# Two more decoder layers: four extra thirds of weight products inside the grouped attention, and another matmul order in the value products

## The reference, cut to what matters

```
u    = rms_norm(h)
proj = u @ w_in                       # dq dk dv | rq rk rv rg | gq gk gv | gates
a = differential_attention(dq, dk, dv)     # 4 heads, values of width 128
r = bidirectional_retention(rq, rk, rv)    # 4 heads, values of width 128, gated by rg
c = grouped_query_attention(gq, gk, gv)    # 8 query heads, 2 key heads
merged = sum over n of sigmoid(gate_n) * (branch_n @ w_branch[n])
h = h + merged @ w_out
h = h + square(relu(rms_norm(h) @ w_mlp_in)) @ w_mlp_out
```

## Time and profile before

| | us |
|---|---|
| median of 3 runs (2966.72 to 2968.79) | 2968.23 |
| the profiled execution, own time | 2965.84 |
| its span, first to last instruction | 2964.0 |
| PE busy in the span | 2915.3 |
| mean granted clock of TensorE | 0.995 of full |

### The profile page before, as it was taken

How to read it: one execution, slowest core, us unless ns; L and a number is a source line. 1 busy time by engine, 2 the same in 40 slices (tenths; PEclk the granted TensorE clock), 3 DMA queues, 4 the chain that set the end, 5 groups by cost and what they waited for, 6 DMA issues and landing times. The chain is left out here.

```text
span 2964.0 us, 36309 instructions
## 1 busy us (share of the span) xinstructions
PE 2915.3 (98%) x13287; PEld 2309.0 (78%) x13287; DVE 1561.3 (53%) x2043; ACT 1276.1 (43%) x1892; POOL 484.3 (16%) x284
## 2 busy tenths in 40 slices
PE   9999999999999999999999999999999999999999
PEld 7787778888788877577777888887667777888887
DVE  4437668345864667656643541445655744553341
ACT  3556325334533446645543431234654554332221
POOL 5002300000100002211112222222221111222121
PEclk9999999999999999999999999999999999999999
DMA  7322213333333332123323333333122322333332
GB/s 192 91 72 70 59 50 97 95 100 94 105 91 101 94 97 67 48 79 89 90 72 93 93 99 94 97 100 100 49 66 72 108 71 78 99 94 98 99 93 93
DMA packets 468595, 263.04 MB, mean 89 GB/s; under 512 B 29674, under 2 KB 457564, under 8 KB 468448
## 3 DMA queue, kind: packets, MB, share of 16 engines
q1 hardware_dynamic: 462512, 250.09, 29.6%
q0 software_dynamic: 5936, 11.03, 1.3%
HBM read 253.70 MB, written 5.64 MB: 87 GB/s over the span
## 5 line engine op out<-in xcount | busy, mean ns | idle before, releaser
L780 POOL TENSOR_TENSOR wL<-wR,wH 128x1024 fp32r<-128x1024 f32 (+1 forms) x165 | 400.6, 2429 | 2265.3 <-ACT wH L742 2265.2
L742 ACT ACTIVATE wH<-wR 128x1024 fp32r<-128x1024 f32 (+3 forms) x472 | 489.0, 1036 | 419.9 <-DMA wR<-in_w_mlp_out_dram 196.5
L747 DVE TENSOR_TENSOR wL<-wR,wH 128x1024 fp32r<-128x1024 f32 (+2 forms) x307 | 372.2, 1212 | 416.3 <-ACT wH L742 392.9
L822 PE MATMUL ps<-uH,wH 128*128 128x512 f32 x1184 | 485.2, 410 | 0.2 <-ACT dts L1732 0.2
L822 PE MATMUL ps<-uL,wH 128*128 128x512 f32 x1184 | 464.8, 393 | 0.0
L809 PE MATMUL ps<-uH,wH 128*128 128x512 f32 x976 | 382.5, 392 | 2.1 <-ACT wH L742 2.1
L809 PE MATMUL ps<-uL,wH 128*128 128x512 f32 x976 | 379.8, 389 | 0.0
L822 PE MATMUL ps<-uH,wL 128*128 128x512 f32 x1184 | 306.8, 401 | 0.0
L822 PEld LDWEIGHTS ps<-uH,wH 128*128 128x128 f32 x1184 | 223.9, 189 | 68.0 <-issue 23.0
L809 PE MATMUL ps<-mH,wH 128*128 128x512 f32 x688 | 267.9, 389 | 0.0
L809 PE MATMUL ps<-mL,wH 128*128 128x512 f32 x688 | 267.7, 389 | 0.0
(11 more groups left out here) (487 smaller groups left out, 4129.0 us busy)
## 6 DMA issues: line engine op xcount, KB each, us to landing
wR<-in_w_in_dram SPq DMA_DIRECT2D x182, 512.0 KB, 3.8
wR<-in_w_mlp_in_dram SPq DMA_DIRECT2D x64, 512.0 KB, 4.0
wR<-in_w_mlp_out_dram SPq DMA_DIRECT2D x64, 512.0 KB, 4.0
wR<-in_ffn_w_up_dram SPq DMA_DIRECT2D x44, 512.0 KB, 3.8
wR<-in_w_branch_dram SPq DMA_DIRECT2D x16, 512.0 KB, 3.4
wR<-in_w_out_dram SPq DMA_DIRECT2D x16, 512.0 KB, 4.1
wR<-in_ffn_w_down_dram SPq DMA_DIRECT2D x16, 384.0 KB, 3.4
wR<-in_ffn_w_down_dram SPq DMA_DIRECT2D x16, 320.0 KB, 3.0
```

What stands on the lines that cost most here:

```text
L742: st.f(st.e.activation(wH[:, slot, 0:n], wR[:, slot, 0:n], ACT.Copy), hi_ready, c + 1)
L747: st.f(st.e.tensor_tensor(wL[:, slot, 0:n], wR[:, slot, 0:n], wH[:, slot, 0:n].bitcast(F32), ALU.subtract), lo_ready, c + 1 if done is Non ...
L780: e.tensor_tensor(wL[:, slot, 0:n], wR[:, slot, 0:n], wH[:, slot, 0:n].bitcast(F32), ALU.subtract).then_inc(sem("lo_pool"), 1)
L822: ins = pe.matmul(o[:, :], w[:, k, :], x[:, k, :], start=s == 0, stop=s == 3 * KD - 1)
```

## The change

In `gqa_steps` the fill behind the transposes takes two thirds instead of one in the four steps with a value product (u = 6, 10, 14, 18), so the grouped attention takes 42 thirds of the stream and not 38, every later step finds the stream up to four thirds further on, and 28 thirds are left behind the retention instead of 32. In `v_pe` the order within a chunk becomes: both high-weight passes of all four token tiles (16 matmuls), then the wait for wL, then the eight low-weight matmuls. A token tile's group is therefore closed in the last eight matmuls of the last chunk.

```diff
 def gqa_steps(score, turned, value, vturn, fill):
@@
         if 2 <= u < 18:
             turned(u - 2)
-        fill(1)
+        fill(2 if u >= 6 and u % 4 == 2 else 1)
         if u == 1:
             vturn()
@@ def v_pe(pe, kind, l, rotated):
             slot = use(pe, (kind, j), l)
-            use_low(pe, (kind, j), l)
             h, lo = wk(wH, slot, kt, cols), wk(wL, slot, kt, cols)
-            for t, g in enumerate(groups):
-                o = g.open(pe) if j == 0 else g.ps
-                for s in range(3 * kt):
-                    k, (w, u) = s // 3, ((h, uH), (h, uL), (lo, uH))[s % 3]
-                    x = j * kt + k
-                    ins = pe.matmul(o[:, 0:cols], u[:, x, t * P:(t + 1) * P], w[:, k, :],
-                                    start=x == 0 and s == 0, stop=x == KD - 1 and s % 3 == 2)
-                    if s == 3 * kt - 1 and j == n - 1:
-                        g.close(ins)
-                    if s == 3 * kt - 1 and j < n - 1 and t == NT - 1:
-                        ins.then_inc(w_part, 1)
-                    if j == 0 and t == NT - 1 and s == 3 * kt - 1:
-                        rope_post_pe(pe, rotated, len(TILES[rotated]) - 1, l)
-                    if (6 * t + s) % THIRD == THIRD - 1:
-                        yield
+            steps = [(t, k, w, u) for t in range(NT) for k in range(kt) for w, u in ((h, uH), (h, uL))]
+            steps += [(t, k, lo, uH) for t in range(NT) for k in range(kt)]
+            for s, (t, k, w, u) in enumerate(steps):
+                g, x = groups[t], j * kt + k
+                first, last = k == 0 and w is h and u is uH, w is lo and k == kt - 1
+                if j == 0 and first:
+                    g.open(pe)
+                if s == 2 * NT * kt:
+                    use_low(pe, (kind, j), l)
+                ins = pe.matmul(g.ps[:, 0:cols], u[:, x, t * P:(t + 1) * P], w[:, k, :],
+                                start=j == 0 and first, stop=j == n - 1 and last)
+                if j == n - 1 and last:
+                    g.close(ins)
+                if s == len(steps) - 1 and j < n - 1:
+                    ins.then_inc(w_part, 1)
+                if j == 0 and s == len(steps) - 1:
+                    rope_post_pe(pe, rotated, len(TILES[rotated]) - 1, l)
+                if s % THIRD == THIRD - 1:
+                    yield
```

## The result

The changed kernel takes 2979.58 us (median of 5 runs, 2979.38 to 2983.63) against 2968.23 before (2966.6 to 2969.62): ratio 1.0045, 95% interval 1.0034 to 1.0055. It is slower by 11.4 us; 2980.5 was predicted. The span of the profiled execution went from 2964.0 to 2977.7 us, 13.7 more, as the one profiled before was on the short side of its runs.

What follows compares the result with a forecast made beforehand. PE's instruction stream was taken as the bound, busy 2915.3 of 2964.0 us. Per layer 6.0 wait + 2.5 clock - 2.3 gain = 6.2, twice 12.4, on 2968.23 gives 2980.6; predicted 2980.5, range 2972.5 to 2987.

Steps and rivals of the forecast that it cites:

- The tail's cover: Behind the retention's last `var`: four thirds gone, PE waits 6.0 us per layer for brL, bounds 4.7 and 7.3.
- The clock: Behind the new wait at the branch chunk: half clock costs 2.5 us per layer, bounds 0 and 3.4.
- The sentence that the edit can only change the 49 us without work: Whole kernel: with no matmul added or removed, only the 49 us in which PE is not busy can change.
- The gain: Grouped attention: added thirds fill waits of PE and win 2.3 us per layer, bounds 0 and 5.7.
- the two short places: Grouped attention's bank rotation: waits of 0.82 and 1.34 us at steps 9 and 12 move to 7 and 11, left standing.
- The value product: New matmul order in the value chunks: nothing won or lost; if the cover is short, up to 2.7 us per layer.
- no new row at line 2840: Value product, table of PE's waits: no new wait there was named as a sign of a right prediction.
- The rival of the shared port: Grouped attention: DVE operations slowed beside POOL's subtractions take back 2.8 us per layer, so no gain; 2985.2 us, chance 0.16.
- The clock did not stay at full: Behind the branch chunk's wait: rival claimed full clock, so 7.4 us slower in all, 2975.6 us; chance 0.13.
- the grouped attention did not give back all its idle time: Waits behind step 6: rival claimed all 5.7 us per layer won, 2973.8 us, just within 0.2%; chance 0.10.

Runs made afterwards that it cites:

- experiment 1: Kernel before plus only the four extra thirds in the grouped attention, value products in the old order: 2980.62 us, ratio 1.0051.
- experiment 2: Kernel before plus only the new order of the value products, one third per step as before: 2967.0 us, ratio 1.0000.
- experiment 3: Changed kernel, but the differential attention gives four thirds back, so 32 are again left behind the retention: 2969.16 us, ratio 1.0011.
- 5: Changed kernel with two extra thirds per layer (steps 6 and 14) instead of four: 2967.89 us, ratio 1.0006.
- experiment 6: Changed kernel, but ScalarE and VectorE handle the last head's norm ahead of the gate chunk ending just before it: 2977.15 us, ratio 1.0039.
- experiment 4: Changed kernel with 22 unused matmuls ahead of the first branch chunk of merge n = 1 in each layer: 2976.85 us, ratio 1.0036.
- experiment 7: Kernel before with four extra thirds at the value products, four fewer in the differential attention, old value-product order: 2964.42 us, ratio 0.9994.
- experiment 8: Kernel before with extra thirds in step 0, behind step 6's transposes, ahead of those of 7 and 11; differential attention four fewer: 2960.99 us, ratio 0.9981.

## Why the prediction was right

**The tail's cover, shown.** The step that decided, four thirds taken from in front of a chain of 7.6 us, held in place and size: 6.0 us forecast, 5.77 measured, twice. The chain itself was 7.63 us against the 7.64 read from the second head; the forecast of 6.0 differs because the profile counts the idle time from the end of the matmul ahead (1583.28 + 0.39) and not from its next start. Experiments 1 and 2 put the loss with the thirds, 3 removes it by giving the cover back, 5 shows that it follows the cover, 6 splits the chain as read.

**The clock, right in kind, too large.** 2.5 us per layer were taken from a gap of 4.76 us; 1.4 and 1.75 were measured (experiment 4). The row gave the length of the half clock from the moment work resumed. In its gap the clock was at 0.83 on average:

```profile
265.60:270.20 4.60, 0.00 (x0) 0.00 (x0) 2.29 (x2) 3.00 (x5) 3.96 (x3) 0.83 0.28 85
```

Here it was at 0.50 for the last 3.0 us of the first layer's wait, so less work fell into the half clock (3.0 and 3.7 us, not 5.0). How much falls behind the wait differs from one place to the next, from 1.4 us to the 2.8 of experiment 6; one row could not give the size, and only the bounds of 0 and 3.4 held. The sentence that the edit can only change the 49 us without work leaves this term out: behind the wait the work itself took longer (0.79 us for the first matmul instead of 0.39).

**The gain, too large as well.** 2.3 us per layer were forecast. The bgL wait of 1.56 us went, and the two short places came back at steps 7 and 11 as counted. But they cost 1.6 to 1.7 us each and not 0.82 and 1.34. PE asks for the bank 4.5 us after the score's start at all four places; what differs is when DVE takes the row maxima of that score. Timelines of PE and of DVE before, for scores 8 and 11:

```profile
1209.04 1.13 PE L3122 MATMUL ps<-qk_g 64*128 64x256 f32 x8 [0.37 <-ACT gpr L3186]
...
1233.56 1.13 PE L3122 MATMUL ps<-qk_g 64*128 64x256 f32 x8
```

```profile
1211.94 1.49 DVE L3220 TENSOR_REDUCE stt<-ps 128x1 f32<-128x512 f32 x2
...
1236.95 1.49 DVE L3220 TENSOR_REDUCE stt<-ps 128x1 f32<-128x512 f32 x2
```

Timelines of PE and of DVE after, for score 10 (score 6 starts at 1195.46, above):

```profile
1229.23 1.14 PE L3125 MATMUL ps<-qk_g 64*128 64x256 f32 x8
```

```profile
1195.26 1.45 DVE L3053 TENSOR_TENSOR qk_d<-raw,cs_d 128x512 f32<-128x512 f32 x1
...
1199.18 1.49 DVE L3223 TENSOR_REDUCE stt<-ps 128x1 f32<-128x512 f32 x2
...
1232.91 1.48 DVE L3223 TENSOR_REDUCE stt<-ps 128x1 f32<-128x512 f32 x2
```

The maxima come 2.90 and 3.39 us after the score's start before, 3.72 and 3.68 after: 0.82 and 0.29 more, and the waits grew by 0.85 and 0.28. Scores 6 and 10 stand in steps with a value product, 8 and 11 do not: after, DVE does bgL (1194.42 and 1228.15) and then the four operations of a "d" tile's rotation (from 1195.26 at score 6) ahead of the maxima. That this order is the reason is read from the rows; no run changed it.

Over both layers the waits behind step 6 sum to 6.7 + 1.8 + 1.1 + 0.5 = 10.1 us (table of waits after; the 3.2 at line 3125 for ACT gpr are step 1) against 11.4 before: 1.3 won, where 4.6 had been forecast. The terms that were off are this one and the clock, and they offset each other in part: 2 x 5.77 + 1.4 + 1.75 - 1.3 = 13.4, against 13.47 between the markers above. So the cover is what the prediction had right; that its sum of 12.4 us came so near is partly luck.

**The value product, priced at nothing.** Its order is worth nothing by itself (experiment 2). What the prediction missed is that banks of the weight chunks rotate too: the wait of 0.55 us for token tile 0's copy comes with the shift (experiment 1), and the earlier opening of the fourth tile's bank costs 0.2 to 0.3 us here and 1.75 where the stream stands differently (3 against 7). So one of the prediction's signs, no new row at line 2840 (now 2843), failed, by 0.5 us in both layers together.

**The rival of the shared port.** Its time, 2985.2, did not come. The gain was nearer to it than to the forecast, and a DVE operation that meets POOL's subtraction stands ahead of the maxima of score 6, 1.45 us long instead of 0.69 (timeline of DVE after, above). The rule of the Trainium skill (SBUF — State Buffer, "Who interferes with whom"), by which a VectorE instruction with two SBUF inputs contends with a GpSimd instruction that reads SBUF, agrees with that length. But the same meeting stands in the timeline of DVE before:

```profile
1195.03 1.41 DVE L3050 TENSOR_TENSOR qk_d<-raw,cs_d 128x512 f32<-128x512 f32 x1
```

In the grouped attention of each layer six DVE operations of two inputs and 512 columns took more than 0.8 us, in both kernels, each beside a subtraction of POOL. Over 0.69 each they lost 10.4 and 10.8 us in the two layers before, 9.4 and 9.7 after. The extra thirds brought no more of these meetings, so they are not what kept the gain small.

**The other rivals.** The clock did not stay at full (windows above), and the grouped attention did not give back all its idle time. Experiment 8 shows that it would have given back more with the thirds elsewhere.

## What to carry to other kernels

Work taken as filling for one stall is cover taken from in front of another: before moving it, find the place where the stream gives it up and compare what is left there with the longest chain that the piece hid (here 9.06 us of cover before and 1.81 after, a chain of 6.4 to 7.6 us). The length of a chain depends on what the engines that follow the stream have to do first, so read it at a place where the same work ends just ahead of it. Put filling ahead of the instruction that waits, by counting the buffer rotation, and take it from a stretch without waits: four thirds so placed, and taken from the differential attention, made the kernel 0.2% faster, where four taken from the tail made it 0.45% slower. With the same source but the places of the change (experiment 7) no difference could be told.

## What the runs showed of the hardware that was not expected

Behind one and the same short wait the granted clock was half in some profiles and full in others. Ahead of step 1 of the second layer PE stood for 1.61 to 1.63 us in nine of the ten profiles (experiment 8 has no wait there). In eight of them the clock stayed at full; in experiment 3 it was half for some 3 us behind the wait (windows of experiment 3, then of before):

```profile
2084.10:2087.30 3.20, 3.20 (x11) 2.52 (x10) 2.73 (x3) 2.88 (x6) 1.79 (x1) 0.50 0.07 13
```

```profile
2084.00:2087.40 3.40, 3.25 (x19) 2.58 (x18) 3.06 (x3) 3.08 (x7) 2.38 (x1) 1.00 0.10 19
```

From this step to the next score it took 7.41 us (2082.41 to 2089.82) instead of 6.21 (2081.65 to 2087.86), so 1.2 us of the profiled run of experiment 3 lie there. A wait of 2.14 to 2.17 us in the first block, which all ten profiles have, was followed by half clock in two of them, experiments 2 and 8 (windows of experiment 8, then of before):

```profile
781.10:783.50 2.40, 2.40 (x6) 1.92 (x7) 2.22 (x3) 1.81 (x3) 0.00 (x0) 0.50 0.31 92
```

```profile
781.10:783.50 2.40, 2.40 (x11) 1.96 (x12) 2.22 (x3) 1.82 (x3) 0.00 (x0) 1.00 0.43 129
```

What decides it, no run here shows.
